# A two-layer hybrid decoder on one core: expert down weights through a staging buffer filled by ScalarE's queue, and three changes of order

## The reference, cut to what matters

```python
for layer in range(DEPTH):                                   # DEPTH = 2
    hn = rmsnorm(x, norm_mix_g[layer])
    proj = hn @ w_in[layer]
    o_a, o_b, o_c = gated_deltanet(...), rwkv7_time_mix(...), stick_breaking_attention(h_sb)
    gates = jax.nn.sigmoid(h_gate)                           # three gates of width 1024
    merged = gates[0] * (o_a @ w_branch_gdn) + gates[1] * (o_b @ w_branch_rwkv) + gates[2] * (o_c @ w_branch_sb)
    x = x + merged @ w_out[layer]
    hn = rmsnorm(x, norm_ffn_g[layer])
    x = x + (swiglu(hn, ...) if layer % 2 == 0 else moe_swiglu(hn, ...))
return rmsnorm(x, final_norm_g)

def moe_swiglu(h, router_w, w_gate, w_up, w_down):           # 8 experts, inner width 3584
    top_vals, top_idx = lax.top_k(tokens @ router_w, 2)
    combine = one_hot(top_idx) * softmax(top_vals)           # summed over the two
    for e in range(8):
        y = (silu(tokens @ w_gate[e]) * (tokens @ w_up[e])) @ w_down[e]
        out = out + combine[:, e:e + 1] * y
```

## Time and profile before

| | before |
|---|---|
| median of 3 runs | 2057.37 us |
| profiled execution | 2054.16 us |
| its span, granted clock | 2052.4 us, 0.984 |
| busy: PE, PEld, DVE, ACT, POOL | 96%, 85%, 19%, 13%, 4% |
| moved in the span | 482.92 MB, mean 235 GB/s |
| loads by one queue (q1) | 481.54 MB, 62.9% of 16 engines |

### The profile page before, as it was taken

The page is one execution under the profiler, slowest core; times in us unless marked ns, Lnnn a source line. Parts: engine busy times, 40 slices in busy tenths (PEclk is TensorE's granted clock), DMA queues, the critical chain, the costliest instruction groups (busy, mean ns, idle before and its releaser), DMA issues.

```text
span 2052.4 us, 66808 instructions
## 1 busy us (share of the span) xinstructions
PE 1962.2 (96%) x31214; PEld 1742.7 (85%) x31214; DVE 392.6 (19%) x948; ACT 271.1 (13%) x579; POOL 88.2 (4%) x174
## 2 busy tenths in 40 slices
PE   7999999999999999999999799999999999999997
PEld 7888887888777788888788799999999898989896
DVE  3335331110000133533211300101000101010001
ACT  1223223000000122222320000000000000000001
POOL 4011101000000001011000000000000000000000
PEclk9999999999999999999999899999999999999999
DMA  7313123467442151311345389999999999999996
GB/s 239 123 44 102 43 84 103 144 207 244 144 144 82 42 160 47 101 45 43 107 139 204 137 335 407 407 407 407 407 407 407 407 407 407 407 407 407 407 407 240
DMA packets 214760, 482.92 MB, mean 235 GB/s; under 512 B 11582, under 2 KB 110092, under 8 KB 214668
## 3 DMA queue, kind: packets, MB, share of 16 engines
q1 hardware_dynamic: 214668, 481.54, 62.9%
HBM read 480.46 MB, written 1.05 MB: 235 GB/s over the span
## 4 chain that ended last, share of the span: by engine, by line
PE 83%; DMA 6%; SPq 4%; DVE 3%; ACT 1%; issue 1%; POOL 0%; DVEq 0%; POOLq 0%
PE bank L1190 29%; PE bank L623 18%; PE bank L1144 7%; DMA pool<-in_moe_w_down_dram 6%; PE bank L713 5%; PE bank L1071 4%; PE bank L1104 4%; SPq L2111 3%; PE bank L1087 3%; PE bank L636 2%; PE bank L677 2%; PE bank L1299 1%; SPq L2116 1%; PE bank L1034 1%; DVE pool L1814 0%
## 5 line engine op out<-in xcount | busy, mean ns | idle before, releaser
L1190 PE MATMUL bank<-pool 128*64 128x80 f32 x21504 | 759.5, 234 | 32.1 <-DMA pool<-in_moe_w_down_dram 23.5
L1190 PEld LDWEIGHTS bank<-pool 128*64 128x64 f32 x21504 | 752.6, 138 | 40.3 <-DMA pool<-in_moe_w_down_dram 25.8
L623 PE MATMUL bank<-hnT,pool 128*128 128x256 f32 x1856 | 431.5, 386 | 6.4 <-DVE pool L1876 6.4
L623 PEld LDWEIGHTS bank<-hnT,pool 128*128 128x128 f32 x1856 | 349.0, 192 | 61.7 <-issue 14.4
L1144 PEld LDWEIGHTS bank<-hnT,pool 128*128 128x128 f32 x640 | 121.6, 190 | 24.6 <-issue 9.1
L1144 PE MATMUL bank<-hnT,pool 128*128 128x256 f32 x640 | 141.2, 379 | 0.0
L2019 DVE TENSOR_TENSOR pool<-pool,bank 128x320 f32<-128x320 f32 x32 | 15.6, 488 | 637.4 <-ACT pool L1584 637.4
L713 PEld LDWEIGHTS bank<-pool 64*64 64x64 f32 x3008 | 94.8, 135 | 17.2 <-issue 11.3
L713 PE MATMUL bank<-pool 64*64 64x32 f32 (+2 forms) x3008 | 103.4, 221 | 2.6 <-DVE pool L1660 1.6
L1584 ACT ACTIVATE pool<-bank 128x320 f32<-128x320 f32 x32 | 14.0, 437 | 675.5 <-PE bank L1190 675.5
L561 POOL TENSOR_TENSOR pool<-pool,level_mask 128x256 f32<-128x256 f32 x72 | 51.9, 736 | 782.1 <-DVE pool L1736 502.1
(11 more groups left out here) (323 smaller groups left out, 1222.4 us busy)
## 6 DMA issues: line engine op xcount, KB each, us to landing
pool<-in_moe_w_up_dram SPq DMA_DIRECT2D x128, 896.0 KB, 16.6
pool<-in_moe_w_gate_dram SPq DMA_DIRECT2D x128, 896.0 KB, 16.6
pool<-in_w_in_dram SPq DMA_DIRECT2D x66, 1024.0 KB, 5.3
pool<-in_moe_w_down_dram SPq DMA_DIRECT2D x64, 1024.0 KB, 16.8
pool<-in_moe_w_down_dram SPq DMA_DIRECT2D x32, 1536.0 KB, 18.6
pool<-in_ffn_w_gate_dram SPq DMA_DIRECT2D x11, 1024.0 KB, 8.5
pool<-in_ffn_w_up_dram SPq DMA_DIRECT2D x11, 1024.0 KB, 5.7
pool<-in_ffn_w_down_dram SPq DMA_DIRECT2D x11, 1024.0 KB, 5.1
```

The source lines that it names most:

```text
L623: ins = mm(ps[:, s * T:(s + 1) * T], w[:, k, (j + s) * P:(j + s + 1) * P], hnT[:, k, :], start=(k == 0), stop=(k == KD - 1))
L1190: ins = mm(bank[rows, cs], w[:, rows], rhs, start=start, stop=stop, skip_group_check=True)
```

## The change

The parts of the change:

- A second set of three down slots. `down_slot(n, 0)` is the stage, into which transfers go, and `down_slot(n, 1)` the place that TensorE reads.
- ScalarE copies stage to place (`down_copy`), once the rows are in the stage and TensorE is done with the round's old ones.
- ScalarE asks for the next rows itself, in its own DMA queue (`stage_load`), right behind the copy: those of the round after next. Round 1's are asked for after the second norm of layer 1.
- SP asks for gate and up rows alone. TensorE waits for ScalarE's copies (`dwn_ready`) and not for the transfers.
- ScalarE's last pass is written out behind the loop, so that it asks for nothing more.
- Attention: four steps, not five, in the second fill of each pair of heads, and gate 0 is copied behind the first pair.
- Norms: the first half is turned before the second is scaled. Dense layer: six tiles kept back, not three.

```diff
+        def down_tiles(n, copy):
+            lo = 2 * KH * HSLOT + copy * FB * D
+            return pool[:, lo + 2 * n * D:lo + min(2 * n + (3 if n == 2 else 2), FB) * D]
+        def down_slot(n, copy=1):
+            return down_tiles(n, copy).rearrange("p (f n) -> p f n", n=D)
...
@@ TensorE, attention, dense_ffn, experts
                     sums(2 * j + 1)
-                    some(steps, 5)
+                    some(steps, 4)
...
-                        if f - 1 >= LAST - 2:
+                        if f - 1 >= LAST - 5:
...
-                                    pe.wait_ge(dwn_loaded[n],
-                                               i * (16 * NR) + j * 16 + 16 * (slot_count[2 * KH + n] + 1))
+                                    pe.wait_ge(dwn_ready, i * (3 * NR) + j * 3 + (dwn_base + n + 1))
...
@@ ScalarE
+            def down_copy(n):
+                A(down_tiles(n, 1), down_tiles(n, 0), ACT.Copy).then_inc(dwn_ready, 1)
+            def stage_load(n, e, r):
+                lo, size = 2 * n * P + r * FB * P, (3 if n == 2 else 2) * P
+                src = a["moe_w_down"][0, e, lo:lo + size, :].rearrange("a (f p) n -> p (a f) n", p=P)
+                act.dma_start(down_slot(n, 0), src).then_inc(dwn_loaded[n], 16)
+            for n in range(3):
+                act.wait_ge(dwn_loaded[n], 16 * (slot_count[2 * KH + n] + 1))
+                down_copy(n)
+            for n in range(3):
+                act.wait_ge(dwn_ready, dwn_base + n + 1)
+                stage_load(n, slice(0, 1), 1)
...
+            def next_load(i, r, n, e):
+                act.wait_ge(dwn_ready, i * (3 * NR) + (3 * r + 3 + dwn_base + n + 1))
+                stage_load(n, e, (r + 2) % NR)
+            def next_down(i, r, n, e0, e1):
+                act.wait_ge(dwn_loaded[n], i * (16 * NR) + 16 * (slot_count[2 * KH + n] + r + 2))
+                if n < 2:
+                    act.wait_ge(dwn_used, i * NR + (r + 1))
+                else:
+                    act.wait_ge(dwn_mm, i * (2 * NR) + (2 * r + down_base + 2))
+                down_copy(n)
+                if r < NR - 2:
+                    next_load(i, r, n, e0)
+                elif e1 is not None:
+                    next_load(i, r, n, e1)
...
                       ACT.Silu).then_inc(he_silu, 1)
+                    if not last or r < NR - 1:
+                        next_down(i, r, 0, e0, e1)
+                        next_down(i, r, 1, e0, e1)
+                        if r < NR - 1:
+                            next_down(i, r, 2, e0, e1)
                 for half in range(2):
                     act.wait_ge(dwn_mm, i * (2 * NR) + (down_base + 2 * NR - 1 + half))
                     A(yT[:, 4 * half:4 * half + 4, :], B[4 + half][:, 0:4 * CAP].rearrange("p (k n) -> p k n", k=4),
                       ACT.Copy).then_inc(yT_ready, 1)
+                if not last:
+                    next_down(i, NR - 1, 2, e0, e1)
                 for half in range(2):
                     act.wait_ge(ye_mm, i * 2 + (half + 1))
...
+            with act.Fori(0, more) as i:
+                one_pass(i, False)
+            one_pass(more, True)
...
@@ VectorE
-                opens = ((), (0, 1), (2,), (3,))
+                opens = ((0,), (1,), (2,), (3,))
...
+                v.wait_ge(vec_ready, l + 1)
+                turned(l, 0, 0)
                 scaled(l, 0, 1)
-                v.wait_ge(vec_ready, l + 1)
-                for t in range(NT):
-                    turned(l, 0, t)
+                turned(l, 0, 1)
...
@@ SP: one round of loads
-                for n in range(3):
-                    if n < 2:
-                        sp_.wait_ge(dwn_used, dwn + 1)
-                    else:
-                        sp_.wait_ge(dwn_mm, dwn * 2 + (down_base + 2))
-                    lo, size = down_rows(n)
-                    down_load(n, bass.ds(e, 1), bass.ds(col + lo, size))
```

More of the change, by code:

```diff
@@ L133, in hidden_slot @@
             return pool[:, n * HSLOT:(n + 1) * HSLOT].rearrange("p (k n) -> p k n", k=2)
-        def down_slot(n):
-            lo = 2 * KH * HSLOT
-            return pool[:, lo + 2 * n * D:lo + min(2 * n + (3 if n == 2 else 2), FB) * D].rearrange("p (f n) -> p f n", n=D)
-        assert 2 * KH * HSLOT + FB * D <= MRING * SLOT
+        def down_tiles(n, copy):
[3 more added lines that the diff above has]
+            return down_tiles(n, copy).rearrange("p (f n) -> p f n", n=D)
+        assert 2 * KH * HSLOT + 2 * FB * D <= MRING * SLOT
         banks = [ctx.enter_context(nc.psum_tensor(f"bank{i}", [P, 512], F32)) for i in range(8)]
@@ L437, in build @@
         he_silu, he_ready, hid_mm, dwn_mm = ff_silu.handle, ff_ready.handle, proj_mm.handle, down_mm.handle
+        dwn_ready, dwn_base = yrs_ready.handle, DEPTH * yrs_ready.per_layer
         yT_ready = sem("yT_ready")
@@ L1579, in _, with one_pass @@
             act.wait_ge(passes_ready, 1)
-            n_pass = act.value_load(pass_expert[0:1, 0:1], min_val=MIN_PASSES, max_val=MAX_PASSES)
-            with act.Fori(0, n_pass) as i:
+            more = act.value_load(pass_expert[0:1, MAX_PASSES + 1:MAX_PASSES + 2], min_val=MIN_PASSES - 1,
+                                  max_val=MAX_PASSES - 1)
+            def next_load(i, r, n, e):
[12 more added lines that the diff above has]
+                    next_load(i, r, n, e1)
+            def one_pass(i, last):
+                e0 = bass.ds(act.value_load(pass_expert[0:1, bass.ds(i + 1, 1)], min_val=0, max_val=NE - 1), 1)
+                e1 = None if last else bass.ds(act.value_load(pass_expert[0:1, bass.ds(i + 2, 1)], min_val=0,
+                                                              max_val=NE - 1), 1)
                 for r in range(NR):
@@ L1911, in dense_ffn @@
                 for t in range(NT):
-                    down_mm.wait(v, 0, down_mm.per_layer - 2 * (1 - t))
+                    down_mm.wait(v, 0, down_mm.per_layer - 3 * (1 - t))
                     for half in range(2):
@@ L2115, in down_load @@
                 src = a["moe_w_down"][0, e, rows, :].rearrange("a (f p) n -> p (a f) n", p=P)
-                sp_.dma_start(down_slot(n), src).then_inc(dwn_loaded[n], 16)
+                sp_.dma_start(down_slot(n, 0), src).then_inc(dwn_loaded[n], 16)
             def down_rows(n):
@@ L2142, in _, with hidden_round @@
             sp_.dma_start(fgain, a["final_norm_g"].partition_broadcast(P)).then_inc(fgain_loaded, 16)
-            def later_round(e, col, hid, dwn):
+            def hidden_round(i, r, e):
+                col = (r + 1) % NR * FB * P
                 for n in range(2 * KH):
-                    sp_.wait_ge(hid_used, hid + (n + 1))
-                    hidden_load(n, bass.ds(e, 1), bass.ds(col, FB * P))
-                for n in range(3):
-                    if n < 2:
-                        sp_.wait_ge(dwn_used, dwn + 1)
-                    else:
-                        sp_.wait_ge(dwn_mm, dwn * 2 + (down_base + 2))
-                    lo, size = down_rows(n)
-                    down_load(n, bass.ds(e, 1), bass.ds(col + lo, size))
-            def rest_of_pass(i, e):
-                with sp_.Fori(0, NR - 1) as j:
-                    later_round(e, j * (FB * P) + FB * P, i * (2 * KH * NR) + j * (2 * KH), i * NR + j)
+                    sp_.wait_ge(hid_used, i * (2 * KH * NR) + (2 * KH * r + n + 1))
+                    hidden_load(n, e, slice(col, col + FB * P))
             more = sp_.value_load(pass_expert[0:1, MAX_PASSES + 1:MAX_PASSES + 2], min_val=MIN_PASSES - 1,
@@ L2165, in _ @@
                 e = sp_.value_load(pass_expert[0:1, bass.ds(i + 1, 1)], min_val=0, max_val=NE - 1)
-                rest_of_pass(i, e)
+                e = bass.ds(e, 1)
+                for r in range(NR - 2):
+                    hidden_round(i, r, e)
+                hidden_round(i, NR - 2, e)
                 e = sp_.value_load(pass_expert[0:1, bass.ds(i + 2, 1)], min_val=0, max_val=NE - 1)
-                later_round(e, 0, i * (2 * KH * NR) + (2 * KH * (NR - 1)), i * NR + (NR - 1))
+                e = bass.ds(e, 1)
+                hidden_round(i, NR - 1, e)
             e = sp_.value_load(pass_expert[0:1, bass.ds(more + 1, 1)], min_val=0, max_val=NE - 1)
-            rest_of_pass(more, e)
+            e = bass.ds(e, 1)
+            hidden_round(more, 0, e)
+            hidden_round(more, 1, e)
+            hidden_round(more, 2, e)
             sp_.wait_ge(fin_ready, 1)
```

## The result

The changed kernel took 2118.86 us, the median of 4 runs (2115.77 to 2120.89), beside 2057.21 for the kernel before on the same chip: ratio 1.0301, 95% interval 1.0283 to 1.0319. The forecast had the sign (2066, slower) and missed the size by 53 us; its range ended at 2076. The profiled span grew from 2052.4 to 2114.0 us, the mean granted clock fell from 0.984 to 0.956. Lines are those of the changed program: experts' matmuls L1195, scatter L1303, gate matmuls of attention L628; down copy L1582, request for stage rows L1588, copies of sums L1639, copies for the scatter L1645; SP's requests L2164.

What follows compares the result with a forecast made beforehand. The expert stage was taken as DMA-bound, with TensorE close behind and the bound ahead of it. Terms of -10.0 (attention), -1.2 (norms) and +20.0 (stage) gave +8.8: 2063.0 profiled, 2066 as median; own range 2058 to 2075, overall 2045 to 2076.

Steps and rivals of the forecast that it cites:

- The bound and the slack: Expert stage: a pass takes 108.2 us of DMA beside 102.5 of TensorE, a slack of 5.6.
- The wait in attention: Both attention layers: of TensorE's 3.20 us idle, 3.0 go, with 1.7 of low clock behind; 5.0 a layer with shorter fills.
- The pass end: End of an expert pass: ScalarE's added copies and requests delay the scatter by 3.1 us in 7 of 8 passes.
- the blocking rival: Pass end: ScalarE's requests block at 2.1 us each as SP's do in a full queue, giving 2100; chance 0.08.
- The displaced loads: Expert pass: down rows in a second queue delay the last up slot to S + 87.2, a wait of 3.5 us.
- The last pass without a load wait: Last expert pass: no late loads compete and no copy delays it, so it runs at TensorE's pace, -5.5 us.
- The rival of more bandwidth: Expert stage loads: two queues move 1% more (0.411), about 9 us in all, giving 2057; chance 0.10.
- The rival in which the lead absorbs all: Expert stage: down loads delay no others, DMA stays the bound at 108.2, giving 2047; chance 0.22.
- the forecast's two: Ends for the load wait in a pass: 4.2 us if queues share bandwidth, 0 if emptied in order of asking.
- Ahead of the stage: Everything before the expert stage: attention -10.0 and norms' order -1.2, together -11.2 us.
- Stage, from pass start to pass start: Expert stage: first pass +6.8, six passes +18.7, last pass -5.5, together +20.0 us.
- the clock term: Expert passes: low clock behind the two added waits, a little over one fall a pass, 1.9 us; ends 0 and 3.4.

Runs made afterwards that it cites:

- e8_half_tail: Changed kernel with half of later rounds' gate and up rows left out and the third down copy and request behind the scatter copies; 2001.87 us, one run.
- e2_tail: Changed kernel with the pass end's third down copy and its request moved behind the two copies for the scatter; 2055.16 us, ratio 0.9993 to the kernel before.
- e6_twoq: Kernel before, with down rows asked for by ScalarE in its own queue, no staging and no copies; 2069.84 us, ratio 1.0066.
- e3_spq: Changed kernel with stage rows asked for by SP in its one queue, behind the same round's gate and up rows; 2042.74 us, ratio 0.9939 to the kernel before.
- e1_front: Kernel before with only the edits ahead of the expert stage, down rows loaded as before; 2043.75 us, ratio 0.9943.
- e7_half: Changed kernel with half of the gate and up rows left out of later rounds' loads, the pass-end wait kept; 2057.3 us, one run.
- e10_half_fill: e7_half with 13 matmuls of zeros on TensorE behind the transposes of a pass end; 2031.96 us, one run.
- e5_copy: Kernel before, one queue, no staging, with added ScalarE copies at the pass end so that TensorE waits ahead of the scatter; 2074.11 us, ratio 1.0089.
- e12_spq_wait: e3_spq with the pass end's second down copy moved behind the copies of sums to lengthen the wait; 2045.87 us, ratio 0.9952 to the kernel before.
- e9_fill: Changed kernel with 13 matmuls of zeros on TensorE behind the transposes of a pass end; 2093.25 us, ratio 1.0192 to the kernel before.

## Why the prediction was wrong

**Right.** The bound and the slack: 108.2 of DMA, 102.4 of TensorE (e8_half_tail). The wait in attention, and the clock behind it at that place. The pass end: +2.9 for +3.1, copies of 1.91 and 2.77, requests of 0.38 for 0.56; the blocking rival is out. The displaced loads: up slot at 87.5 (e2_tail) for 87.2. The last pass without a load wait. The rival of more bandwidth is out (407 GB/s in the fullest slices of e6_twoq). The rival in which the lead absorbs all holds for one queue alone: e3_spq gives 2042.7 where that rival had 2047. The trace agrees with what the Trainium skill (DMA: Bandwidth & Descriptors, Queues, rings and completion order) says of turns between queue rows: the load wait is there (3.5 us in e2_tail), at the end of the forecast's two that follows from sharing, and is gone with the second queue (at most 0.9 us in e3_spq).

**The sum by its terms.** Ahead of the stage: forecast -11.2; the first experts' matmul behind the gather stands at 1175.18, 7.5 sooner. The two low stretches behind the waits in attention are gone, but others are longer (at 60 and 84 the clock was low for 6.8 us, not 3.4), so of the 3.4 us that the forecast took for the clock this execution shows nothing. In e1_front, where those two last 3.4 us, the matmul stands at 1171.86, 10.8 sooner. Stage, from pass start to pass start: forecast +6.8, +18.7, -5.5; measured +10.8 (117.1 against 106.3), +62.4 (709.7 against 647.3), -4.1 (98.8 against 102.9). Together +69.1 instead of +20.0, and 69.1 less 7.5 is the 61.6 of the span.

**The step that failed** is the clock term, "I take a little over one fall a pass, 1.9 us", with its upper end of 3.4 for two. There are two falls in each of the six passes. Take the fourth: 119.9 - 102.4 - 2.9 (pass end) - 5.0 (loads) leaves 9.6 us. Over the six passes the mean step is 118.1 and the load waits are 4.9, so that 7.9 are left, against 1.9: some 36 us of the miss of 53. (The rest is 8 in those passes' load waits, 5 in the first and the last pass and 4 ahead of the stage.) I had read the price of a fall off a row where the clock came back after 3.4 us. In the stage it comes back after 10 to 14 us at a pass end, which costs 4.3 to 6.0 us a fall (e7_half, e10_half_fill). And I had put the chance of a fall by waits of 2.1 us (seven of them, not eight, two with a fall), where the pass-end waits are 3.2 us and brought it every time (e5_copy, e7_half). The trace of before already had rows of a long fall, at 0.50 for these 15 us just ahead of the first pass, where TensorE does short pieces of work between waits:

```profile
1165.00:1170.00 5.00, 2.11 (x10) 2.01 (x11) 2.58 (x16) 0.20 (x1) 0.00 (x0) 0.50 0.10 40
1170.00:1175.00 5.00, 1.88 (x9) 1.78 (x9) 2.74 (x18) 0.00 (x0) 0.00 (x0) 0.50 0.00 0
1175.00:1180.00 5.00, 2.92 (x44) 2.92 (x46) 3.72 (x17) 0.51 (x1) 0.00 (x0) 0.50 0.02 5
```

**A second step**, smaller: the load wait of 3.5 us was taken as fixed. With full buffers and the clock up it is near (3.5 for the up slot and 0.9 for the gate slot in the pass shown of e2_tail). In the changed kernel the pass begins at 1.2 GHz, the first request goes out at 1532.66, 5.4 us after the pass's first matmul and not 3.5, the DMA engines stand still meanwhile, and the up slot comes after 91.2 us instead of 87.5. So the low clock behind one wait lengthens the next.

```profile
1532.66 0.38 SPq L2164 DMA_DIRECT2D pool<-in_moe_w_gate_dram  x1
```

**Why either cure is enough.** The changed kernel exceeds e2_tail by 64 us and e3_spq by 76, and these are not two losses to add: there is one slack of 5.8 us a pass. With one queue the pass end's wait and fall go into it, since the loads run on and the load waits shrink: nearly all of it in e12_spq_wait (steps of at most 108.6), all but 1.4 us a pass in e5_copy (109.6). With two queues and no wait at the pass end, the load waits and their fall fill it and stand out by 1.1 us (109.3 in e2_tail). With both, nothing shrinks, and a pass is 102.4 + 2.9 + 4.9 + 7.9 = 118.1. The load wait seems to be set by what has shared the DMA engines since the pass began, not by how much has been moved in all; its place (87.5 to 91.2 us into the pass) fits that, and no run tests it alone.

**Open.** What makes the clock stay low for 10 to 14 us behind a pass end and for 3.4 to 10.2 behind a load wait was not tried; the work behind them differs (scatter and transposes with gaps of 0.7, against dense matmuls). Nor is it shown why a wait of 2.34 us brought a fall in four passes and not in the other three, or why one load wait of 3.42 in e6_twoq brought none.

## What to carry to other kernels

Where two engines are within some per cent of each other, price the waits that a change adds together with the clock behind them, and take that price from a row in the stage where they will stand. When DMA is near the bound, first try loads of different urgency in one queue in the order of need: a helper's queue may move rows early and hand the delay to rows that are wanted now. A head start counts only if what lands last has little work behind it.

## What the runs showed of the hardware

Behind waits of 3.15 to 3.37 us at a pass end the granted clock fell to 0.50 every time (15 of 15 in e5_copy and e7_half) and came back after 10 to 14 us, but for the last of e5_copy, where the program ends. Behind 2.34 us it fell in 4 of 7 (e12_spq_wait), behind 1.47 with a filler ahead in 2 of 7 (in each of e9_fill and e10_half_fill), behind 1.15 or less in none (e3_spq). Behind load waits of 2.6 to 3.7 us in dense matmuls the low stretch was 3.4 to 10.2 us, but for one of 3.42 in e6_twoq, which brought none. A filler of 1.93 us of matmuls of zeros stopped five of seven falls. Two queues moved no more than one: 407 GB/s in the fullest slices of e6_twoq, as before. A request of ScalarE cost 0.38 us, while some of SP's in the same stage of the changed kernel, with loads of its own still under way, cost 1.9 to 6.2.
